# Layer 1's gate and output blocks: one 512-column product of the high weights with both activation parts

## What is computed

```python
h, gate = modulate(x, norm_g, (c_act @ w_ada + b_ada)[:, None, :])
u = h @ w_in
...
y_conv = conv_branch(u[..., OFF_CONV_GLU:OFF_CONV_GATE], u[..., OFF_CONV_GATE:OFF_LRU_GATE], ...)
y_lru = y_lru * jax.nn.silu(u[..., OFF_LRU_GATE:OFF_Q])
...
x = x + gate * (jnp.concatenate([y_conv, y_lru, y_attn], axis=-1) @ w_out)
```

## Time and profile before

| | |
|---|---|
| median of 3 runs | 1262.2 us (1261.91 to 1263.3) |
| span of the profiled execution | 1262.1 us; no other time of this execution is listed |
| TensorE busy | 97% |
| TensorE weight loads | 77% |
| VectorE busy | 63% |
| ScalarE busy | 43% |
| mean DMA rate | 187 GB/s |
| mean granted TensorE clock | 0.993 of full speed |

### The profile page before, as it was taken

The page is one execution under the profiler, slowest core; times in us unless marked ns, Lnnn a source line. Parts: engine busy times, 40 slices in busy tenths (PEclk is TensorE's granted clock), DMA queues, the critical chain, the costliest instruction groups (busy, mean ns, idle before and its releaser), DMA issues.

```text
span 1262.1 us, 16910 instructions
## 1 busy us (share of the span) xinstructions
PE 1225.4 (97%) x6838; PEld 975.6 (77%) x6838; DVE 794.3 (63%) x1252; ACT 543.5 (43%) x857; POOL 9.8 (1%) x11
## 2 busy tenths in 40 slices
PE   3999999999999999999999999999999999999996
PEld 1555776666777777776778888989888988899995
DVE  5444556766756667763465555696799977656554
ACT  5222445542223433355342222355775455575542
POOL 0000100000000000000000000000000000000000
PEclk9899999999999999999999999999999999999998
DMA  9999756555764444333446666433332544325542
GB/s 335 350 348 348 228 189 232 221 201 204 266 246 167 142 142 166 129 111 142 153 165 231 221 225 225 151 134 133 136 107 101 196 144 150 119 103 205 189 167 67
DMA packets 80894, 236.36 MB, mean 187 GB/s; under 512 B 9392, under 2 KB 54192, under 8 KB 59440
## 3 DMA queue, kind: packets, MB, share of 16 engines
q1 hardware_dynamic: 80816, 235.27, 52.5%
HBM read 230.54 MB, written 2.10 MB: 184 GB/s over the span
## 4 chain that ended last, share of the span: by engine, by line
PE 94%; DMA 2%; DVE 2%; SPq 1%; ACT 1%; issue 0%; DVEq 0%; ACTq 0%
PE psum_block L789 23%; PE psum_block L790 22%; PE psum_block L791 22%; PE psum_ada L629 4%; PE psum_ada L666 2%; PE psum_scores L816 2%; PE psum_scores L717 1%; PE psum_scores L866 1%; PE psum_scores L853 1%; PE psum_scores L719 1%; PE psum_scores L718 1%; PE psum_scores L886 1%; SPq L578 1%; DMA glu<-in_w_ada 1%; DMA raw<-in_w_ada 1%; PE psum_block L913 1%
## 5 line engine op out<-in xcount | busy, mean ns | idle before, releaser
L789 PE MATMUL psum_block<-h_hi,w_hi 128*128 128x256 f32 (+1 forms) x1648 | 562.1, 341 | 0.3 <-DVE h_lo L1346 0.3
L790 PE MATMUL psum_block<-h_lo,w_hi 128*128 128x256 f32 (+1 forms) x1648 | 553.4, 336 | 0.0
L791 PE MATMUL psum_block<-h_hi,w_lo 128*128 128x256 f32 (+1 forms) x1648 | 553.2, 336 | 0.0
L1354 DVE TENSOR_TENSOR w_lo<-raw,w_hi 128x1024 fp32r<-128x1024 f32 x210 | 254.7, 1223 | 332.7 <-ACT w_hi L1006 332.4
L1006 ACT ACTIVATE w_hi<-raw 128x1024 fp32r<-128x1024 f32 x210 | 220.3, 1057 | 444.0 <-PE psum_block L791 409.5
L789 PEld LDWEIGHTS psum_block<-h_hi,w_hi 128*128 128x128 f32 x1648 | 312.7, 190 | 61.8 <-issue 26.9
L790 PEld LDWEIGHTS psum_block<-h_lo,w_hi 128*128 128x128 f32 x1648 | 312.9, 190 | 32.7 <-issue 1.9
L791 PEld LDWEIGHTS psum_block<-h_hi,w_lo 128*128 128x128 f32 x1648 | 312.8, 190 | 32.6
L1623 DVE SCALAR_TENSOR_TENSOR Y<-glu,small,Y 128x512 f32<-128x512 f32 (+1 forms) x240 | 130.4, 612 | 0.0
L1163 ACT ACTIVATE T<-psum_scores,stats 128x512 f32<-128x512 f32 (+1 forms) x48 | 29.0, 616 | 46.5 <-DVE stats L1671 46.5
L629 PE MATMUL psum_ada<-raw,cstat 128*32 128x512 f32 x384 | 47.8, 600 | 0.0
(11 more groups left out here) (212 smaller groups left out, 1193.3 us busy)
## 6 DMA issues: line engine op xcount, KB each, us to landing
raw<-in_w_blocks SPq DMA_DIRECT2D x105, 1024.0 KB, 4.9
raw<-in_w_ada SPq DMA_DIRECT2D x81, 1024.0 KB, 6.8
qreg<-in_w_blocks SPq DMA_DIRECT2D x8, 896.0 KB, 11.5
glu<-in_w_ada SPq DMA_DIRECT2D x5, 1024.0 KB, 11.6
kv<-in_w_ada SPq DMA_DIRECT2D x5, 1024.0 KB, 11.9
bd<-in_w_ada SPq DMA_DIRECT2D x5, 1024.0 KB, 11.9
Y<-in_xT SPq DMA_DIRECT2D x8, 512.0 KB, 8.1
T<-in_xT SPq DMA_DIRECT2D x16, 256.0 KB, 5.2
```

The costliest lines, as they stand in the source:

```text
L789: mm(ps[:, cols], hi, hh[:, k, t], start=(at == 0), stop=False)
L790: mm(ps[:, cols], hi, hl[:, k, t], start=False, stop=False)
L791: last = mm(ps[:, cols], lo, hh[:, k, t], start=False, stop=(at == DT - 1))
L1354: V.tensor_tensor(wl[:, u % 4, 0:n], raw_of(item)[:, cols], wh[:, u % 4, 0:n].bitcast(F32), ALU.subtract).then_inc(*C.up("lo", u))
```

## The change

For the lg, cg and out blocks of layer 1 (`apart`), the first two of the three products of a k tile become one. Its weights are the high part; its moving operand is both activation parts side by side, 2 x 256 columns, and it writes the whole bank: high times high in columns 0 to 255, high times low in columns 256 to 511. The third product, low weights times high activations, still goes to columns 0 to 255 alone. `h_hi` and `h_lo` become two halves of one tensor `h_parts`. What was summed within PSUM has now to be added when the bank is read: for lg and cg VectorE adds the halves into `tbuf[:, 256:512]` with a `tensor_reduce`, and both the tanh and the multiplication read that; for out blocks VectorE adds the upper half, times the gate, to Y, and then the lower half as before. No step of the DMA queue and no weight rounding changes.

```diff
-        hh = sb("h_hi", [P, DT, TOK], F32R)
-        hl = sb("h_lo", [P, DT, TOK], F32R)
+        parts = sb("h_parts", [P, 2, DT, TOK], F32R)
+        hh, hl = parts[:, 0, :, :], parts[:, 1, :, :]
...
+        def apart(l, b):
+            return l == 1 and BLOCKS[l][b][0] in ("lg", "cg", "out")
...
+                    if apart(l, b):
+                        mm(segs(ps), hi, parts[:, :, k, t], start=(at == 0), stop=(at == DT - 1))
+                        last = mm(ps[:, cols], lo, hh[:, k, t], start=False, stop=(at == DT - 1), skip_group_check=True)
+                        continue
                     mm(ps[:, cols], hi, hh[:, k, t], start=(at == 0), stop=False)
                     mm(ps[:, cols], hi, hl[:, k, t], start=False, stop=False)
                     last = mm(ps[:, cols], lo, hh[:, k, t], start=False, stop=(at == DT - 1))
...
                 elif kind in ("lg", "cg"):
-                    if (kind, i) != ("lg", 0):
+                    if apart(l, b):
+                        act.wait_ge(*C.at("both_parts", gb))
+                        ps = tbuf[:, LAT:TOK]
+                    elif (kind, i) != ("lg", 0):
                         act.wait_ge(*C.at("evac_dve", gb - 1))
                     fn(tbuf[:, 0:n], ps, ACT.Tanh, scale=0.5).then_inc(*C.up("gate_tanh", gb))
...
                 elif kind in ("lg", "cg"):
+                    if apart(l, b):
+                        dve.wait_ge(*C.at("mm", unit(0, gb, 1)))
+                        dve.wait_ge(*C.ago("evac_dve"))
+                        V.tensor_reduce(tbuf[:, LAT:TOK], bank(gb).rearrange("p (s t) -> p t s", t=LAT), axis=AX.X, op=ALU.add
+                                        ).then_inc(*C.up("both_parts", gb))
+                        ps = tbuf[:, LAT:TOK]
                     dve.wait_ge(*C.at("gate_tanh", gb))
...
+                    if apart(l, b):
+                        stt(Y[:, i, 0:LAT], bank(gb)[:, LAT:TOK], ada[:, l, 0, GATE * DT + i:GATE * DT + i + 1], Y[:, i, 0:LAT], ALU.mult, ALU.add
+                            ).then_inc(*C.up("low_part", gb))
+                        dve.wait_ge(*C.ago("low_part"))
                     for s in range(n // LAT):
```

## The result

The changed kernel takes 1271.0 us (1267.7 to 1272.0, 4 runs) against 1262.1: 1.0067 of the time before, interval 1.0055 to 1.008, which is 8.5 us slower by the ratio (9.0 by the two medians). The forecast was 1266.4 with a range to 1270.5. Its sign and its five waits held. The size, +4.2, was half of what came: the clock fell in two of the waits, which the forecast had only as a rival and entered at nothing, and that is most of the other half.

The account below looks back on a forecast made before the run. The prediction took TensorE, full at 2.4 GHz through the output blocks, as the bound. Waits of 8.8 less 5.1 saved plus 0.5 in the tail gave +4.2 on 1262.2: 1266.4 us, range 1262.5 to 1270.5.

Parts of the forecast that it names:

- five waits: TensorE waits before block 35 0.98, product with V 1.99, pointwise product 0.92 and 2.78, block 40 2.10; sum 8.8 us.
- the clock: Rival: TensorE's clock falls in the new waits, up to +3.4 us, so 1268 to 1270; chance 0.18.
- The joined stream: TensorE, 384 k tiles in 24 blocks: 346.7 ns each in place of 360.0, 5.1 us saved; bounds 0 to 26.7 ns.
- The reduce: New VectorE operation after each gate block, 512 PSUM elements to 256: 0.69 us, bounds 0.42 and 1.22.
- Tanh from SBUF: ScalarE's tanh in gate blocks, reading the reduce's output: 0.42 us in place of 0.37.
- The table load behind the later of two waits: Block 34, ScalarE: with two waits the tanh's table load no longer runs ahead, 1.28 us more.
- The tail: Last output block: nothing hides its second evacuation, 0.5 us on the path.
- a fallen clock between 1120 and 1170: Sign in the profile, in us of the trace, that would show the forecast wrong.
- The mild version: Rival: table load ahead of its wait (-1.3) and reduce of 0.55 (-1.0): +1.9, 1264.1 us; chance 0.20.
- the one with no waits: Rival: the waits do not reach TensorE, block 35's bank margin holds; 4.6 us gained, 1257.6; chance 0.11.
- a dearer reduce: Rival: reduce of 1.2 us, reading two far halves of a bank: +7.7, 1269.9 us; chance 0.05.
- an unchanged stream: Rival: the stream gets hardly cheaper, 1.0 us gained in place of 5.1; 1269.5 us; chance 0.04.

Follow-up runs that it names:

- e1: Changed kernel with joined products kept but both evacuations as before, upper halves of the banks never added: 1257.1 us, ratio 0.996.
- e2: Changed kernel with the longer evacuations kept but separate 256-column products, joined only in a block's first and last k tile: 1272.1 us, ratio 1.0075.
- e6: Changed kernel with joined products and new evacuation in the eight lg and cg blocks alone, output blocks as before: 1272.3 us, ratio 1.0081.
- e5: Changed kernel with the gate blocks' reduce moved ahead of the second weight residue lo(gb+2, 1) in VectorE's queue: 1261.9 us, ratio 0.9994.
- e7: Changed kernel with the gate blocks' tanh waiting for the reduce alone, no longer for the products too: 1267.4 us, ratio 1.0041.
- e3: Changed kernel with idle TensorE products, 12 ahead of pointwise group 2's wait and 9 ahead of block 40's: 1267.8 us, ratio 1.0045.
- e11: Changed kernel, joined only in cg blocks and output blocks 40 to 54, reduce ahead of lo(gb+2, 1), tanh behind reduce alone: 1258.1 us, ratio 0.9975.
- e4: Changed kernel with joined products and second addition in the 16 output blocks alone, lg and cg as before: 1260.5 us, ratio 0.9992.
- e8: Kernel with joined output blocks alone, its high and low activation parts 2 KB apart in place of 32 KB: 1260.7 us, ratio 0.9989.
- e9: Changed kernel with joined products in output blocks 40 to 54 only, gate blocks and last block as before: 1260.3 us, ratio 0.9991.
- e10: Kernel joined in output blocks 40 to 54 only, odd k tiles (last excepted) putting the low weights' product first: 1259.2 us, ratio 0.998.

## Why the prediction was wrong, point by point

- **The joined stream**, forecast 5.1 saved. Right in kind, a little too large. In the profile of the changed kernel some 12.5 of 48 halves step at 0.353, which leaves 4.4. The forecast knew only the pace of 0.347. Its interval of 0 to 26.7 ns per k tile held; 6.7 and 13.3 both occur. e1 measured 5.0 by its ratio, of which its own profile shows 2.5. The Trainium skill, page "TensorE: Matmul & The Clock Gate", section "Back-to-back issue gap", gives columns/2.4 plus 2.5 ns, and calls it the gap of an isolated product. An estimate from that figure is 325.0 ns for a pair of these products and 327.5 for three of 256 columns. Measured in this stream are 347 or 353 and 360, so the rule does not hold for it.
- **The reduce**, forecast 0.69: it took 0.68. Tanh from SBUF, forecast 0.42: 0.42.
- **The walk's five waits**, forecast 0.98, 1.99, 0.92, 2.78 and 2.10, sum 8.8. By starts: block 35, 1116.21 less 1113.19 and the 1.67 of the transposes, 1.35; the product with V, 1120.83 less 1118.76 and a pair of 0.35, 1.7; pointwise group 0, 1129.84 less 1127.19 and 1.73, 0.9; group 2 2.7; block 40 2.1. Sum 8.8. The steps were right in place and releaser, and each in size to within 0.4. That the sum agrees to 0.1 is in part luck: block 35's wait was 0.4 longer and the next 0.3 shorter than forecast. e2 and e6 show that the evacuation of gate blocks makes them, e5 that it does so by its place in the queue.
- **The table load behind the later of two waits**: right, shown by e7 from the other side. The forecast's remark on the page "ScalarE: Activation LUTs" of the Trainium skill, section "What ACT_TABLE_LOAD costs", needs a correction: of its 2.66 us the section puts 1283 ns on the load itself, with which the rows agree (1.28), and the rest on a drain. No row here shows the drain; the load from 1123.14 ends where its activation starts, 1124.43.
- **The tail**, forecast 0.5: the last block's two additions start at 1254.90 and 1255.42, so 0.5, and the wait of L692 grew from 0.6 to 1.1.
- **The clock**: this is the step that failed. The forecast entered nothing for it and gave the rival 0.18, because its longest wait was 2.8 us and the fall in the earlier trace rows came some 3 us after the last product. That comparison was wrong in kind, not only narrow: the clock fell behind both of the longer waits, 2.7 and 2.1 us, and it did so after TensorE had started again, 3.5 and 2.8 us after the product before the wait. So a wait shorter than 3 us was no protection. The falls cost 1.6 and 1.7 us. Together: 8.8 - 4.4 + 3.3 + 0.5 = 8.2, of 8.5 measured. e3 shows the cause. The forecast had named this sign itself: "a fallen clock between 1120 and 1170".
- **The rivals.** The mild version and the one with no waits are out; so are a dearer reduce and an unchanged stream. The last had a slip in it: 216 ns for two passes, less 213.3, are 2.9 (from 1.73/8) for both and 1.5 for one, so 0.6 us would have been its gain and not 1.0. What was forecast as a rival "up to +3.4, so 1268 to 1270" is what happened, with a total near its full price. How it came about differs: the rival had the whole pointwise half at the lower level, and in fact it was half of that and as much again in block 40. My range ended half a microsecond under the median, as it took the rival's sum for an edge.
- **What stays open.** In which waits the clock falls varies between executions: both in the changed kernel's profile, the first alone in e2 and e7, the second alone in e6. By the starts these eight waits are 1.8 to 2.7 us long. A fall followed five of them, the shortest 2.1, and none followed one of 2.7 in e6. That fits the spread of the changed kernel's runs (1267.7 with a mean clock of 0.994, 1272.0 with 0.991), but one profile of each kernel is too few to give a chance.

## What to carry to other kernels

Where an evacuation is made longer, walk every queue that it stands in: 0.7 us of new work in each of eight blocks cost 8.8 us of waits because it stood behind two weight residues on one engine and ahead of the roundings and copies on another, and moving it by one place in one queue gave all of the loss back. When such a walk ends in TensorE waits of two microseconds or more, price a fall of its clock with them as part of the forecast and not as a rival: here 1.6 to 1.7 us each, behind five of eight waits of 1.8 to 2.7 us. A join of two products saves at most the fixed part of a product, here 6.7 or 13.3 ns a k tile, so it is worth making only where the addition that it needs later has room. In e11 that was so for the output blocks but the last and for the cg blocks; the lg blocks with the edits of both e5 and e7 were not tried.

## What the runs showed of the hardware that I had not expected

- The stream of one 512-column and one 256-column f32r product for each k tile has two paces at full clock, 0.353 and 0.347 us, and keeps one of them until the stream is broken: 0.353 in all output blocks of e1, e3, e4, e5, e7, e8 and e9, 0.347 in those of e11 and in the changed kernel after its second fall of the clock. Streams of one width alone did not show it: 0.120 and 0.227 in the earlier trace rows. Neither the distance of the two runs (e8) nor the order alone (e10, 0.349) settles what chooses the pace. At the lower level of the clock a pair takes 0.64 us (1170.56 to 1171.20), which is 768 columns at 1.2 GHz with nothing over.
- The granted clock fell after waits of 2.1 and 2.7 us and not after those of 1.1 and 1.2 (e5) or those of 1.4 and 1.7 in the changed kernel itself. In the four profiles with a fall it came 0.8 to 1.1 us after TensorE had started again, and each of the five falls lasted about 3.4 us (0.66 over 5 us).
- A table load runs ahead of an activation's wait when that wait is the only one, and behind it when there are two (block 34 in e7 against the changed kernel): 1.28 us on or off the path for one redundant semaphore wait.
